# A decoder layer with a mixture of experts on one core: expert rows fetched one transfer per token tile, group maxima taken inside the normalisation loop, and a row broadcast issued behind the last router product

## The chip, the cores and the metric

The kernel runs on one core of one Trainium2 chip. The metric is the device time of one execution in microseconds; the median of the runs is quoted, and the profile comes from one execution of its own.

## What is computed

One hybrid decoder layer on 512 tokens of width 1024, in float32. The part up to the first normalisation is attention and a short convolution, joined by an output projection. After it:

```python
x = layer_norm(alpha * x + gate1 * mix, ln1_g, ln1_b)
h2 = x * (1 + scale2) + shift2
g = argmax(h2 @ w_router_group + b_router_group)        # 1 of 4 groups
e0, e1 = top 2 of the 8 experts of that group, by h2 @ w_router_expert + b
moe = sum over the two experts of weight * ((silu(h2 @ w_gate) * (h2 @ w_up)) @ w_down)
out = layer_norm(alpha * x + gate2 * moe, ln2_g, ln2_b)
```

There are 32 experts with 3 MB of weights each.

## The kernel before

Tokens are cut into four tiles of 128. Each engine has its own program, written out by hand, and they meet at semaphores.

**Output projection and first normalisation.** TensorE computes the projection in nine pieces (`project_out`, L1549; eight products of 512 or 256 columns each). VectorE takes each piece with `mix` (L1039). In a loop over the tiles (L1075 to L1099) it takes the moments, asks GpSimd for a power (`inv_std`, L613: the inverse deviation), computes the centred and scaled rows into `h2nat` meanwhile (L1081), waits for the power, and writes `h2p` (L1091). The last tile is written in two halves. ScalarE stores `h2p` to memory (`store_h2`, L808), normalises `xs` (L813) and copies the transposed rows out of PSUM into `h2T` (L829, L840 for the halves of the last tile).

**Router.** TensorE turns the rows (`transpose_h2`, L1560) and multiplies them by the router weights (`route`, L1570: eight products of 40 columns, two TensorE instructions each). Its order at the end of this stage, L1589 to L1602: transpose 0, projection piece 6, route 0, transpose 1, pieces 7 and 8, transpose 2, route 1, `spread_row(6)`, route 2, transpose 3, route 3. `spread_row` (L1542) is one 512-column product with a matrix of ones; it broadcasts half a row of `gate2` over the partitions and `row_out` (L795) on ScalarE copies it out. Rows 0 to 6 come before the choice of experts, row 7 after it.

VectorE chooses with `choose(first, n)` (L1102): first for tiles 0 to 2 together, then for tile 3. It adds the bias into `lg` (L1105), takes the group maximum and its index (L1108, L1111), masks the other groups, takes the two best experts, and ends with `mb` (L1129), the hot rows. TensorE sums these into positions (L1608), VectorE builds a table of slots (L1174 to L1178), TensorE multiplies it (L1618), VectorE turns the result into row numbers (L1164 to L1167), and GpSimd gathers the rows of the first expert pair (L627). TensorE fills that time with `spread_row(7)` and three more broadcasts whose results nobody reads (L1624). VectorE then finishes `xs` of tiles 3 and 2 (L1193, L1197), which signals `x1_last`.

**Weights.** SyncE issues all weight loads (L464 to L478) from a ring of 8 gate/up buffers of 2 MB (issued as two halves) and 6 down buffers of 1 MB. At the end of the router stage its order is: the load of expert 5 after the last logits (L503), the second half of buffer 7 after `x1_last` (L505), down weights 5, then expert 8 once the first expert's gate products are done.

**Experts.** Sixteen pairs; each expert takes gate/up products (L1640), a transpose, down products (L1649). Results go to `ysb`, and GpSimd scatters them to `y_dram`, whose row 2t + k holds token t's k-th expert.

**Tail.** When the last scatter but one has landed, SyncE loads the expert rows of each tile in the order 1, 2, 3, 0, one transfer of 512 KB for each of the two k (L541 to L544), with a semaphore for each. VectorE adds them to `x1`: `first_terms(1, 2)`, `(2, 2)`, `(3, 2)`, `(0, 1)` (L1359), each waiting for half k just before using it. TensorE adds the last pair's rows (L1759) and the partial sums (L1766), and for tile 0 also its second half (L1773). The statistics and the second normalisation follow, tile 1 on ScalarE and GpSimd, tiles 2, 3 and 0 on VectorE, and the output is stored.

Of the kernel before, what the change touches and what calls it, by code (L numbers as in the profile page):

```python
# [96 lines left out]
def layer_kernel(nc, x, c, w_ada, b_ada, w_in, conv_w, w_out, ln1_g, ln1_b, w_router_group,  # L97
# [3 lines left out]
    with ctx:  # L101
# [6 lines left out]
        def sem(name):  # L108
            return ctx.enter_context(nc.semaphore(name))
# [113 lines left out]

        lg = rtm("lg", [P, TC, NR])
        lem = rtm("lem", [P, TC, NE])
        g_top, e_top = rtm("g_top", [P, TC, 8]), rtm("e_top", [P, TC, 8])
        g_idx, e_idx = rtm("g_idx", [P, TC, 8], U32), rtm("e_idx", [P, TC, 8], U32)
        not_g = rtm("not_g", [P, TC, NG])
# [33 lines left out]
        ld_x1 = [sem(f"ld_x1{i}") for i in range(TC)]  # L262
        ld_y = [[sem(f"ld_y{i}{k}") for k in range(2)] for i in range(TC)]
        st_h2 = [sem(f"st_h2{n}") for n in range(2)]
# [144 lines left out]
        def _(sp):  # L409
# [131 lines left out]
            for i in TAIL:  # L541
                for k in range(2):
                    sp.dma_start(y_tok[i][:, k], y_dram.rearrange("(i p k) n -> i k p n", p=P, k=2)[i, k]
                                 ).then_inc(ld_y[i][k], 16)  # L544
            out_rows = out[0].rearrange("(i p) n -> i p n", p=P)
# [169 lines left out]
        def _(act):  # L715
# [103 lines left out]
            for i in range(TC - 1):  # L819
# [10 lines left out]
                if i == 1:  # L830
                    act.wait_ge(x1_done, 1)
                    store_x1(1)
            row_out(6)
            act.wait_ge(h2_done, TC + 1)
            store_h2(TC - 1)
            for half in range(2):
# [3 lines left out]
                s.copy(h2T_of(TC - 1)[:, ks].rearrange("p k t -> p (k t)"), flat[:, half * 512:(half + 1) * 512]).then_inc(h2t_ev, 1)  # L840
            normal(TC - 1)
            act.wait_ge(gap_done, 1)
            s.activation(g4[:, 1], g4[:, 0], ACT.Exp).then_inc(gap_exp, 1)
# [83 lines left out]
        def _(dve):  # L927
# [7 lines left out]
            def settle():  # L935

                dve.wait_ge(dve_did, count[0])
# [129 lines left out]
            def moments(n):  # L1067
# [5 lines left out]
                w.tensor_scalar(var_e[:, n:n + 1], mv[:, n, 1:2], EPS, None, ALU.add).then_inc(var_done, 1)  # L1073

            for i in range(TC):  # L1075
                wait(dve, h2_done, i)
                mix(TC + i)
                if i == TC - 1:
# [3 lines left out]
                                           op0=ALU.subtract, op1=ALU.mult))  # L1082
                if i >= 2:
                    dve.wait_ge(st_h2[i % 2], 16)
                    dve.wait_ge(h2t_done, i - 1)
# [16 lines left out]
            def choose(first, n):  # L1102

                tiles = slice(first, first + n)
                link(w.tensor_tensor(lg[:, tiles], ps[:, 2 + first // 3, first % 3 * NR:(first % 3 + n) * NR].rearrange("p (c e) -> p c e", c=n),  # L1105
                                     b_r[:].unsqueeze(1).to_broadcast([P, n, NR]), ALU.add))
                for i in range(first, first + n):
                    did(w.max(out=g_top[:, i], in_=lg[:, i, 0:GPAD]))  # L1108
                settle()
                for i in range(first, first + n):  # L1110
                    did(w.max_index(out=g_idx[:, i], in_max=g_top[:, i], in_values=lg[:, i, 0:GPAD]))  # L1111
                settle()
                link(w.tensor_tensor(not_g[:, tiles], iota[:, 0:NG].unsqueeze(1).to_broadcast([P, n, NG]),
# [17 lines left out]
            dve.wait_ge(h2_done, TC + 1)  # L1131
            dve.wait_ge(ld_br, 32)
            dve.wait_ge(pads, 2)
            dve.wait_ge(logit_done, TC - 1)
# [224 lines left out]
            def first_terms(i, n):  # L1359

                dve.wait_ge(ld_x1[i], 16)
                for k in range(n):
                    dve.wait_ge(ld_y[i][k], 16)
                    ins = w.scalar_tensor_tensor(out=x1_rows_of(i), in0=y_tok[i][:, k], scalar=wk[:, k, i:i + 1],
                                                 in1=x1_rows_of(i), op0=ALU.mult, op1=ALU.add)
                    if k + 1 < n:
                        link(ins)
                ins.then_inc(partial, 1)
# [22 lines left out]
        def _(pe):  # L1391
# [178 lines left out]
            def route(i, halves=1):  # L1570
                for half in range(halves):
                    pe.wait_ge(h2t_ev, i + 1 + half)
                    for k in range(half * KC // halves, (half + 1) * KC // halves):
                        ins = t.matmul(ps[:, 2 + i // 3, i % 3 * NR:(i % 3 + 1) * NR], h2T_of(i)[:, k], w_r[:, k],
                                       start=k == 0, stop=k == KC - 1)
                ins.then_inc(logit_done, 1)
# [18 lines left out]
            transpose_h2(2)  # L1595
            route(1)
            pe.wait_ge(gate2_moved, 1)
            pe.wait_ge(mixg_done, 2 * TC - 1)
            spread_row(6)
            route(2)  # L1600
            transpose_h2(3, halves=2)
            route(3, halves=2)  # L1602

# [158 lines left out]
            def other_terms(i, by_pe):  # L1762
# [7 lines left out]
                if by_pe:  # L1770
                    pe.wait_ge(ld_y[i][1], 16)
                    for n in range(2):
                        t.matmul(ps[:, sum_bank(i) + n], diag[:, i, 1], y_tok[i][:, 1, n * 512:(n + 1) * 512],  # L1773
                                 start=False, stop=True).then_inc(summed, 1)
# [36 lines left out]
```

## Time and profile before

| | |
|---|---|
| median of 3 runs | 551.34 us (550.74 to 553.63) |
| the profiled execution's own time | 551.43 us |
| its span, first to last instruction | 549.7 us |
| mean granted TensorE clock | 0.979 |
| TensorE busy | 509.2 us, 93% |
| VectorE busy | 285.4 us, 52% |
| HBM read / written | 159.60 MB / 17.30 MB, 322 GB/s over the span |

How to read the rows further down: times are microseconds from the start of the span. In the chain of waits each line is a piece of the one chain that ended last: start, length, what. In a timeline a line is a group of instructions that run on without a break: start, length, engine, line of the kernel, operation, output and input, count, and in brackets how long the engine was idle before it and what ended that. TensorE matmuls are listed with their start and a modelled end, so two groups in a row overlap a little. PEclk is the granted TensorE clock, 1.00 for 2.4 GHz and 0.50 for 1.2 GHz. SPq is SyncE issuing a transfer, ACTq is ScalarE doing so.

### The profile page before, as it was taken

Reading aid. Unit: us, or ns where it says so; the run is one execution under the profiler, and the core shown is the slowest. Engines: PE = TensorE matmul, PEld = TensorE weight load, DVE = VectorE, ACT = ScalarE, POOL = GpSimd, SP = SyncE. Lnnn points to the kernel's source line nnn. Section 1 sums busy time; section 2 is a strip of 40 time slices with the busy share of each in tenths; the row PEclk is TensorE's granted clock in tenths of the full one; section 3 lists DMA queues with packets and bytes.
Section 4 is the critical chain, followed back from the end, with each engine's and each line's share of the span. In section 5 each row is a group of like instructions: output and inputs, shape, how many; then the busy total and the mean of one; then the engine's idle time right before and its main releaser. Section 6 shows DMA issues by size and latency. Waiting matters only on the chain.

```text
span 549.7 us, 6477 instructions
## 1 busy us (share of the span) xinstructions
PE 509.2 (93%) x2516; PEld 275.4 (50%) x2516; DVE 285.4 (52%) x520; ACT 105.5 (19%) x173; POOL 102.8 (19%) x112
## 2 busy tenths in 40 slices
PE   3999999999999999999996999999998798899883
PEld 2445468744444444444584555555554354444531
DVE  4675999664946393263888732232222222213388
ACT  1000211233122321100232311111111111122020
POOL 2000000061316040030452111111211021111115
PEclk9999999999999999999996999999999999979997
DMA  8999779944640254269998999999999999999863
GB/s 258 357 360 352 229 240 317 317 172 153 229 154 1 78 171 158 66 258 418 410 385 317 397 407 422 414 415 418 415 416 419 414 415 416 416 417 416 308 239 153
DMA packets 71296, 169.22 MB, mean 308 GB/s; under 512 B 7918, under 2 KB 45858, under 8 KB 63072
## 3 DMA queue, kind: packets, MB, share of 16 engines
q1 hardware_dynamic: 64304, 152.22, 73.4%
q10 hardware_dynamic: 2480, 8.44, 4.0%
q0 software_dynamic: 4480, 8.12, 3.9%
q8 instruction: 21, 0.34, 0.2%
q14 instruction: 11, 0.09, 0.0%
HBM read 159.60 MB, written 17.30 MB: 322 GB/s over the span
## 4 chain that ended last, share of the span: by engine, by line
PE 75%; DVE 9%; DMA 9%; SPq 3%; issue 3%; ACT 1%; POOL 0%; DVEq 0%; POOLq 0%; ACTq 0%
PE ps L1640 17%; PE ps L1510 11%; PE ps L1556 10%; PE ps L1649 8%; PE ps L1421 8%; PE ps L1480 5%; DMA w_gu<-in_w_up_dram 5%; PE ps L1630 3%; PE ps L1473 2%; DMA y_tok<-y_dram 2%; PE ps L1499 2%; PE ps L1544 2%; SPq L466 1%; DVE acc_rows L954 1%; DMA xs<-in_x_dram 1%
## 5 line engine op out<-in xcount | busy, mean ns | idle before, releaser
L1640 PE MATMUL ps<-w_gu,xT 128*64 128x256 f32 x1024 | 119.4, 386 | 6.0 <-issue 3.1
L1640 PEld LDWEIGHTS ps<-w_gu,xT 128*64 128x64 f32 x1024 | 72.4, 138 | 43.5 <-issue 5.8
L1510 PE MATMUL ps<-hT,w_stage 128*128 128x512 f32 x192 | 84.8, 595 | 0.0
L1275 DVE TENSOR_TENSOR ysb<-ps,rows_gate 64x512 f32<-64x512 f32 x64 | 44.1, 688 | 58.6 <-PE ps L1649 58.1
L1649 PE MATMUL ps<-w_dn,hidT 128*64 128x512 f32 x256 | 61.4, 599 | 6.3 <-issue 5.6
L1266 DVE TENSOR_TENSOR hid<-ps,silu_sb 128x128 f32<-128x128 f32 x32 | 9.3, 292 | 94.3 <-ACT silu_sb L865 94.3
L954 DVE SCALAR_TENSOR_TENSOR acc_rows<-ada_stage,csil,acc_rows 128x256 f32<-128x256 f32 x112 | 55.2, 493 | 4.0
L1510 PEld LDWEIGHTS ps<-hT,w_stage 128*128 128x128 f32 x192 | 35.5, 190 | 41.0 <-issue 41.0
L1556 PE MATMUL ps<-wo,mixT 128*128 128x512 f32 (+1 forms) x144 | 55.6, 545 | 0.0
L1421 PE MATMUL ps<-hT,w_first 128*128 128x512 f32 x96 | 45.9, 625 | 0.9 <-DVE hT L980 0.9
L1556 PEld LDWEIGHTS ps<-wo,mixT 128*128 128x128 f32 x144 | 27.2, 190 | 27.1 <-issue 26.3
L640 POOL DMA_INDIRECT y_dram<-ysb,slot_row x14 | 14.2, 1012 | 141.2 <-DVE ysb L1275 141.2
L1649 PEld LDWEIGHTS ps<-w_dn,hidT 128*64 128x64 f32 x256 | 17.0, 136 | 29.1 <-issue 24.6
L865 ACT ACTIVATE silu_sb<-ps 128x128 f32<-128x128 f32 x32 | 8.9, 278 | 114.0 <-PE ps L1640 114.0
L1421 PEld LDWEIGHTS ps<-hT,w_first 128*128 128x128 f32 x96 | 18.2, 199 | 20.0 <-issue 20.0
L1480 PE MATMUL ps<-w_stage,hT 128*128 128x256 f32 x128 | 27.8, 379 | 0.0
L1002 DVE TENSOR_TENSOR_SCAN stay<-stay,block_end 128x1280 f32<-128x1280 f32 x8 | 24.1, 3014 | 4.2 <-POOL stay L592 4.2
L1480 PEld LDWEIGHTS ps<-w_stage,hT 128*128 128x128 f32 x128 | 24.3, 190 | 3.7 <-issue 0.5
L589 POOL TENSOR_SCALAR_AFFINE_SELECT stay<-stay 128x384 f32<-128x384 f32 x8 | 5.3, 659 | 100.5 <-ACT stay L746 100.5
L627 POOL DMA_INDIRECT xg<-h_dram,slot_tok x16 | 16.9, 1054 | 37.1 <-PE ps L1640 23.1
L966 DVE SCALAR_TENSOR_TENSOR acc_cols<-ada_in,csil,acc_cols 128x512 f32<-128x512 f32 (+1 forms) x35 | 22.6, 645 | 1.5 <-DMA ada_in<-in_w_ada_dram 0.2
L1044 DVE TENSOR_TENSOR h2nat<-ps,rows_gate 128x512 f32<-128x512 f32 (+1 forms) x9 | 5.7, 631 | 25.1 <-PE ps L1556 25.0
(221 smaller groups left out, 513.5 us busy)
## 6 DMA issues: line engine op xcount, KB each, us to landing
w_gu<-in_w_gate_dram SPq DMA_DIRECT2D x32, 1024.0 KB, 19.9
w_gu<-in_w_up_dram SPq DMA_DIRECT2D x32, 1024.0 KB, 23.0
w_dn<-in_w_down_dram SPq DMA_DIRECT2D x32, 1024.0 KB, 24.5
ada_stage<-in_w_ada_dram SPq DMA_DIRECT2D x16, 1024.0 KB, 6.3
w_stage<-in_w_in_dram SPq DMA_DIRECT2D x9, 1024.0 KB, 8.4
ada_in<-in_w_ada_dram SPq DMA_DIRECT2D x12, 512.0 KB, 9.4
y_dram<-zeros ACTq DMA_DIRECT2D x4, 1024.0 KB, 5.8
wo<-in_w_out_dram SPq DMA_DIRECT2D x2, 2048.0 KB, 12.1
```

Source lines behind the costliest of these rows:

```text
L627: g.indirect_dma_start(out=buf[:], out_offset=None, in_=h2_dram, in_offset=bass.IndirectOffsetOnAxis(ap=slot_tok[:, j:j + 1], axis=0), bou ...
L954: link(w.scalar_tensor_tensor(out=acc, in0=st[:, k], scalar=csil[:, 3, k:k + 1], in1=acc, op0=ALU.mult, op1=ALU.add))
L966: ins = w.scalar_tensor_tensor(out=acc, in0=ada_in[c][:, k], scalar=csil[:, 3, k:k + 1], in1=acc, op0=ALU.mult, op1=ALU.add)
L1002: w.tensor_tensor_scan(out=st[:, 0:ZW][:, ::-1], data0=st[:, 0:ZW][:, ::-1], data1=block_end[:, ::-1], initial=1.0, op0=ALU.mult, op1=ALU. ...
L1275: ins = w.tensor_tensor(to[e * HD:(e + 1) * HD, b * 512:(b + 1) * 512], ps[b * HD:(b + 1) * HD, down_bank(y), :], gate2r[b * HD:(b + 1) * ...
L1421: ins = t.matmul(ps[:, n], w_first[:, k, n * P:(n + 1) * P], hT[:, k], start=k == 0, stop=k == KC - 1)
L1480: ins = t.matmul(dst[:, 0:CW], hT[:, k, i * P:(i + 1) * P], st[:, k], start=k == 0, stop=k == KC - 1)
L1510: ins = t.matmul(ps[:, 6], st[:, k, (f % 2) * P:(f % 2 + 1) * P], hT[:, k], start=k == 0, stop=k == KC - 1)
L1556: ins = t.matmul(ps[:, 4 + q % 4, 0:width], mixT[:, i, k], wo[n][:, k, col:col + width], start=k == 0, stop=k == KC - 1)
L1630: ins = t.transpose(flat[:, ROWS_AT + k * P:ROWS_AT + (k + 1) * P], by_channel(xg[rows_buffer(j)])[:, k], ident[:])
L1640: ins = t.matmul(ps[a * SLOTS:(a + 1) * SLOTS, GATE_BANK[e], 0:2 * P], rows_in[:, k, e * SLOTS:(e + 1) * SLOTS], weights[:, :, k, a * P:(a ...
L1649: ins = t.matmul(ps[b * SLOTS:(b + 1) * SLOTS, bank, :], hidT[e][:, a * SLOTS:(a + 1) * SLOTS], weights[:, a, b * 512:(b + 1) * 512], star ...
```

## The change

Three edits. (1) The expert rows of a tile come in one transfer of 1 MB, with one semaphore, instead of two of 512 KB; `first_terms` waits for it before its first use. (2) The group maximum of one tile becomes a function `group_top`. It is called for tile 0 in the loop at i = 2 and for tile 1 at i = 3, behind the computation of `h2nat` and ahead of the wait for the power; `choose` calls it for its last tile only (tile 2, then tile 3). For this the buffers `lg`, `g_top` and `g_idx` get a place of their own, the waits for the bias move ahead of the loop, and the logits of even tiles go to PSUM bank 2, of odd tiles to bank 3. (3) `spread_row(6)` moves on TensorE from behind route 1 to behind route 3, and `row_out(6)` on ScalarE from ahead of the last tile's copies to behind `normal(3)`.

```diff
-        lg = rtm("lg", [P, TC, NR])
+        lg = sm("lg", [P, TC, NR])
...
-        g_top, e_top = rtm("g_top", [P, TC, 8]), rtm("e_top", [P, TC, 8])
-        g_idx, e_idx = rtm("g_idx", [P, TC, 8], U32), rtm("e_idx", [P, TC, 8], U32)
+        g_top, e_top = sm("g_top", [P, TC, 8]), rtm("e_top", [P, TC, 8])
+        g_idx, e_idx = sm("g_idx", [P, TC, 8], U32), rtm("e_idx", [P, TC, 8], U32)
...
             for i in TAIL:
-                for k in range(2):
-                    sp.dma_start(y_tok[i][:, k], y_dram.rearrange("(i p k) n -> i k p n", p=P, k=2)[i, k]
-                                 ).then_inc(ld_y[i][k], 16)
+                sp.dma_start(y_tok[i][:], y_dram.rearrange("(i p k) n -> i p k n", p=P, k=2)[i]).then_inc(ld_y[i], 16)
...
-            row_out(6)
             act.wait_ge(h2_done, TC + 1)
             store_h2(TC - 1)
...
             normal(TC - 1)
+            row_out(6)
             act.wait_ge(gap_done, 1)
...
+            def group_top(i):
+
+                link(w.tensor_tensor(lg[:, i], ps[:, 2 + i % 2, i // 2 * NR:(i // 2 + 1) * NR], b_r[:], ALU.add))
+                link(w.max(out=g_top[:, i], in_=lg[:, i, 0:GPAD]))
+                link(w.max_index(out=g_idx[:, i], in_max=g_top[:, i], in_values=lg[:, i, 0:GPAD]))
+
+            dve.wait_ge(ld_br, 32)
+            dve.wait_ge(pads, 2)
             for i in range(TC):
...
                 if i >= 2:
+                    dve.wait_ge(logit_done, i - 1)
+                    group_top(i - 2)
                     dve.wait_ge(st_h2[i % 2], 16)
...
-                link(w.tensor_tensor(lg[:, tiles], ps[:, 2 + first // 3, first % 3 * NR:(first % 3 + n) * NR].rearrange("p (c e) -> p c e", c=n),
-                                     b_r[:].unsqueeze(1).to_broadcast([P, n, NR]), ALU.add))
-                for i in range(first, first + n):
-                    did(w.max(out=g_top[:, i], in_=lg[:, i, 0:GPAD]))
-                settle()
-                for i in range(first, first + n):
-                    did(w.max_index(out=g_idx[:, i], in_max=g_top[:, i], in_values=lg[:, i, 0:GPAD]))
-                settle()
+                group_top(first + n - 1)
...
                 dve.wait_ge(ld_x1[i], 16)
+                dve.wait_ge(ld_y[i], 16)
                 for k in range(n):
-                    dve.wait_ge(ld_y[i][k], 16)
...
             transpose_h2(2)
             route(1)
+            route(2)
+            transpose_h2(3, halves=2)
+            route(3, halves=2)
             pe.wait_ge(gate2_moved, 1)
             pe.wait_ge(mixg_done, 2 * TC - 1)
             spread_row(6)
-            route(2)
-            transpose_h2(3, halves=2)
-            route(3, halves=2)
```

## Rows read from the trace of the kernel before

**Rows 1.** Chain of waits, expert stage: start us, us, what.

```profile
440.01 25.28 DMA w_gu<-in_w_up_dram
```

**Rows 2.** Chain of waits, end of projection to the first expert rows.

```profile
281.95 0.88 PE ps L1567 x8
...
284.54 0.93 PE ps L1544 x2
285.47 1.73 PE ps L1574 x16
...
287.32 0.29 DVE lg L1105
...
290.72 0.12 DVE lg L1105
...
292.62 0.17 DVE mb L1129
...
295.71 2.01 PE ps L1544 x2
```

**Rows 3.** SyncE's own waits, 280 to 306 us: total, times, longest.

```profile
SPq L466 <- DVE ps L1197: 9.8, 1, 9.8
```

**Rows 4.** Timeline, all engines, last tile's rows and logits.

```profile
283.79 1.28 DVE L1081 SCALAR_TENSOR_TENSOR h2nat<-xs,mv,rows_a 128x1024 f32<-128x1024 f32 x1
283.95 1.52 POOL L613 TENSOR_TENSOR rstd<-var_e,mh 128x1 f32<-128x1 f32 x1 [4.50 <-DVE var_e L1073]
285.68 1.41 DVE L1091 SCALAR_TENSOR_TENSOR h2p<-h2nat,rstd,rows_b 128x512 f32<-128x512 f32 x2 [0.62 <-POOL rstd L613]
287.13 0.33 ACTq L809 DMA_DIRECT2D h_dram<-h2p  x1
287.73 1.07 ACT L840 COPY h2T<-ps 128x512 f32<-128x512 f32 x2 [1.63 <-PE ps L1567]
288.36 1.98 PE L1574 MATMUL ps<-w_r,h2T 128*128 128x40 f32 x16 [0.23 <-ACT h2T L840]
291.35 0.16 DVE L1113 TENSOR_TENSOR not_g<-iota,g_idx 128x4 f32<-128x4 f32 x1
...
295.16 0.22 ACT L843 ACTIVATE g<-g 128x16 f32<-128x16 f32 x1 [3.93 <-DVE g L1180]
```

**Rows 5.** Windows: us, PE, PEld, DVE, ACT, POOL busy, PEclk, DMA share, GB/s.

```profile
290.00:291.00 1.00, 0.34 (x4) 0.22 (x2) 0.90 (x6) 1.00 (x1) 0.00 (x0) 0.83 0.98 279
...
300.00:301.00 1.00, 1.00 (x3) 0.42 (x2) 1.00 (x2) 0.00 (x0) 0.44 (x1) 0.55 0.46 172
...
481.50:482.00 0.50, 0.50 (x2) 0.07 (x1) 0.00 (x0) 0.38 (x1) 0.42 (x1) 0.81 1.01 418
```

**Rows 6.** Chain of waits, one-row broadcasts of the second norm's rows.

```profile
479.35 4.83 PE ps L1690 x8
```

**Rows 7.** Timeline, SyncE's loads of the expert rows and VectorE's first two terms.

```profile
516.52 6.14 SPq L543 DMA_DIRECT2D y_tok<-y_dram  x8
...
524.70 1.29 DVE L1364 SCALAR_TENSOR_TENSOR x_back<-y_tok,wk,x_back 128x1024 f32<-128x1024 f32 x1
...
526.83 1.28 DVE L1364 SCALAR_TENSOR_TENSOR x_back<-y_tok,wk,x_back 128x1024 f32<-128x1024 f32 x1 [0.85 <-DMA y_tok<-y_dram]
```

**Rows 8.** Line 543, the last of the eight loads: duration ns, start; issue to landing.

```profile
L543 SPq DMA_DIRECT2D y_tok<-y_dram x1: 933/933/933, 521.7 to 521.7; - x1
...
DMA to landing us min/median/max: 12.6/12.6/12.6
```

**Rows 9.** Chain of waits in the tail.

```profile
528.30 1.30 DVE x_sb L1364
...
533.34 1.28 DVE x_back L1364
```

**Rows 10.** Windows in the tail, columns as in rows 5.

```profile
524.00:526.00 2.00, 1.28 (x3) 0.68 (x4) 1.95 (x2) 0.00 (x0) 0.00 (x0) 1.00 1.01 297
526.00:528.00 2.00, 2.00 (x6) 0.76 (x4) 1.17 (x1) 0.00 (x0) 0.00 (x0) 1.00 1.00 389
```

More of the change, by code:

```diff
@@ L222, in rtm @@
             return at(name, shape, o, dt)
-        lg = rtm("lg", [P, TC, NR])
+        lg = sm("lg", [P, TC, NR])
         lem = rtm("lem", [P, TC, NE])
-        g_top, e_top = rtm("g_top", [P, TC, 8]), rtm("e_top", [P, TC, 8])
-        g_idx, e_idx = rtm("g_idx", [P, TC, 8], U32), rtm("e_idx", [P, TC, 8], U32)
+        g_top, e_top = sm("g_top", [P, TC, 8]), rtm("e_top", [P, TC, 8])
+        g_idx, e_idx = sm("g_idx", [P, TC, 8], U32), rtm("e_idx", [P, TC, 8], U32)
+        assert base + small[0] <= nc.sbuf_usable_end
         not_g = rtm("not_g", [P, TC, NG])
@@ L262, in layer_kernel @@
         ld_x1 = [sem(f"ld_x1{i}") for i in range(TC)]
-        ld_y = [[sem(f"ld_y{i}{k}") for k in range(2)] for i in range(TC)]
+        ld_y = [sem(f"ld_y{i}") for i in range(TC)]
         st_h2 = [sem(f"st_h2{n}") for n in range(2)]
@@ L1131, in _ @@
             dve.wait_ge(h2_done, TC + 1)
-            dve.wait_ge(ld_br, 32)
-            dve.wait_ge(pads, 2)
             dve.wait_ge(logit_done, TC - 1)
@@ L1573, in route @@
                     for k in range(half * KC // halves, (half + 1) * KC // halves):
-                        ins = t.matmul(ps[:, 2 + i // 3, i % 3 * NR:(i % 3 + 1) * NR], h2T_of(i)[:, k], w_r[:, k],
+                        ins = t.matmul(ps[:, 2 + i % 2, i // 2 * NR:(i // 2 + 1) * NR], h2T_of(i)[:, k], w_r[:, k],
                                        start=k == 0, stop=k == KC - 1)
@@ L1770, in other_terms @@
                 if by_pe:
-                    pe.wait_ge(ld_y[i][1], 16)
+                    pe.wait_ge(ld_y[i], 16)
                     for n in range(2):
```

## The prediction

> **What bounds the kernel now.** I read the chain of waits first, then the windows with the granted clock, then the timelines of the two stretches that the change touches.
>
> In the expert stage the chain rests on weight loads; the longest piece is one of 25.28 us [rows 1]. A delay of TensorE alone is swallowed there. What is not swallowed is the moment at which the stream of loads starts again after the router. SyncE waited 9.8 us for VectorE's last sum of `xs` before it could issue the second half of buffer 7 [rows 3], and the transfer engines are only half busy meanwhile, at 300 to 301 [rows 5]. That sum hangs on the choice of experts. So a microsecond in the choice is a microsecond at the end, through the stream of loads.
>
> In the router the chain runs on TensorE to the end of route 2 at 287.20, then through VectorE's two choices: tiles 0 to 2 from 287.32, tile 3 from about 290.64 (the second addition into `lg` overlaps the end of the first choice), `mb` ready at 292.79 [rows 2]. The logits of tile 3 ended at 288.36 + 1.98 = 290.34 [rows 4]: 0.3 us before they were needed. Of the 3.3 us of the first choice, then, little more than 0.3 can be taken away before route 3 decides.
>
> In the tail VectorE adds seven blocks of 1.28 us; it waited 0.85 us for tile 1's second half [rows 7], and from 528.30 on it goes at its own pace, 5.04 us for four blocks, to 533.34 [rows 9].
>
> **The change, part by part.**
>
> *Group maxima in the loop.* One tile's addition, maximum and index take VectorE from 290.64 to 291.35, 0.71 us [rows 2, 4]. At i = 3 `h2nat` ends at 285.07 and the power at 285.47, `h2p` starts at 285.68 [rows 4]: a hole of 0.62 us. With the addition overlapping the end of `h2nat` by 0.08, as it does in rows 2, `group_top` ends at 285.70. The hole covers all but some hundredths; I take 0.05 for each of the two calls, 0.1 in all, at most 0.2. The power itself is covered by nothing new: GpSimd starts it before. Queued behind the new wait for logits is `h2p`, but route 1 ended at 284.54 [rows 2], before `h2nat` does. Route 0 is earlier still, and the bias landed before the loop. In `choose` two of three tiles' maxima go: about 0.5 us, plus 0.2 because it may start at the end of `h2p`.
>
> *The broadcast behind route 3.* Route 2 moves up by 0.93 us, to 284.54 to 286.27 [rows 2]. Transpose 3 no longer stands behind it but waits for `h2p`: first half at 286.4 + 0.1. ScalarE can copy only after it has issued the store of `h2p`, at 287.13 + 0.33, about 287.5 [rows 4], where it copied at 287.73. Route 3 thus starts 0.2 us earlier at best. With the 0.1 from above, the choice of tile 3 starts at 290.3 instead of 290.64: a gain of 0.3 us. The bound is then route 3, with VectorE waiting for it. The broadcast itself (0.93 us) hides in the 2.5 us in which TensorE waits for `mb`. On ScalarE the copy of row 6 now stands ahead of the exponential, which ran at 295.16 after ScalarE had waited 3.93 us for VectorE [rows 4]; that wait covers it. SyncE's load of expert 5 waits for route 3 too, and goes with it.
>
> *The clock, which this reordering touches.* The granted clock fell from 2.4 to 1.2 GHz at 290.66 (0.83 in the window 290 to 291) and came back at 300.9 [rows 5]. Before the fall TensorE had done nothing wider than 128 columns since the broadcast ended at 285.47, 5.2 us earlier [rows 2]. Between the router and the tail it fell once more, at 481.81 (0.81 in the window 481.5 to 482), 2.5 us after TensorE had begun the one-row broadcasts of the second norm [rows 5, 6]. In the new order the broadcast no longer stands between routes 1 and 2: the last wide product ends at 281.95 [rows 2]. Then come a transpose, route 1, route 2, transpose 3 and route 3, all narrow. With the longer of the two lags the clock falls at 287.2, with the shorter at 284.5. Either is ahead of route 3. I take 287.2, from the row nearest to this case in kind.
>
> What does it cost? No row shows the 40-column products at 1.2 GHz. Nothing at all is the lower bound, twice the time the upper. The same two 512-column instructions took 0.93 us at the high clock and 2.01 at the low [rows 2], so I take twice. The first half of transpose 3 stays fast. The second starts at 287.2 and takes 0.85 us instead of 0.43, the last copy ends near 289.0, which still leads its half of route 3. Route 3: start 288.15, 2 × 1.71 = 3.42 us, and the 0.27 us by which the modelled end lags [rows 2, 4]: 291.85. The choice of tile 3 starts at 292.0 instead of 290.64: **+1.3 us**. `mb` comes at 294.1; the broadcast, now slow, ends at about 293.3 and still hides. The gather and the broadcasts that fill its time move with VectorE.
>
> *One transfer per tile.* VectorE's first block of tile 1 ran at 524.70 while the second half was under way [rows 7]; now both blocks start when the whole tile is there. Where does it land? If 1 MB lands when its second half did, at 526.83, tile 2 starts at 526.83 + 2.52 = 529.35 instead of 528.30: +1.05 us [rows 7, 9]. Tile 0 must be there whole, too: its second half landed at 521.7 + 12.6 = 534.3 [rows 8], while VectorE took its first half at 533.34 [rows 9]: +1.0 again, at the same place, so not added. The other bound: in 524 to 526 the engines were fully busy but moved 297 GB/s, afterwards 389 [rows 10]. If larger pieces take away that slow time, the tile lands at about 525.1 and VectorE gains 0.7 us. The second of these rows shows that today's pieces run fast as well once the slow time is over, so I stay above the middle and take **+0.5**. Four issues of 0.8 us on average (6.14 for eight) go from SyncE [rows 7], but the first one starts as before, and the later ones were not what the data waited for.
>
> The Trainium skill, page "DMA: Bandwidth & Descriptors", section "Rules for kernel authors", asks for at least 1 MiB in a DMA for the best bandwidth and for many small transfers to be joined. By that rule the merged load would land earlier, and the tail term would be the lower bound instead of the one taken.
>
> *Sum*: 551.43 + 1.3 + 0.5 = **553.2 us**. The profiled execution stands 0.09 above the median of the three runs, so the same number serves against either.
>
> **The rivals.**
>
> *The clock holds through route 3.* For it: the fall before came only after route 3, when TensorE already stood still, so that the idle time and not the narrow work may have brought it. Then the router gives -0.3, the tail +0.5: 551.6. Chance 0.24.
>
> *The transfer gains.* The slow time in rows 10 goes and tile 1 lands at 525.1: router +1.3, tail -0.7, so 552.0 (550.4 where the clock holds too). Against it: the tail's last loads landed about as fast as VectorE used them. Chance 0.18. The skill's rule above speaks for this one.
>
> *Slower: the clock falls during route 2.* With the short lag, as in rows 5 and 6, it falls at 284.5 to 284.8. Route 2 then ends at 287.7, the transposes at 289.45, the first copy at 289.5, route 3 at 289.5 + 3.42 + 0.27 = 293.2; the choice of tile 3 starts at 293.3, +2.65. With the tail: 554.6. It decides if the fall comes before 286.27, the end of route 2. Chance 0.15.
>
> *The change does nothing that shows.* The two effects are too small beside the spread of the runs, or the stream of loads takes up the router's delay: -0.3 to +0.5, 551.4. Against it: SyncE's wait [rows 3]. This shares the first rival's numbers; chance 0.05.
>
> The forecast itself has 0.38.
>
> **How the numbers follow.** Half a per cent, 2.8 us, is about what a measurement of this kernel can tell from no change. The forecast and three rivals lie inside it. Slower takes about 0.12 of the early fall and 0.05 of the forecast (the clock term at its worst with +1.0 in the tail gives 554.0 and above). Faster would need over 548.6; only the transfer rival with both favourable terms comes near, 0.03. The range goes from 550.4, that pair, to 554.8, the early fall.
>
> **What would show it.** In the windows PEclk at 0.50 from about 287 and route 3 taking about 3.5 us; VectorE idle for about 2 us ahead of the second choice, released by L1574; `x1_last` and the load behind it 1.3 us later; in the tail VectorE idle from 524.7 (plus the shift) until the first tile lands, then seven blocks nearly without a break. The forecast is wrong if PEclk is 1.00 until 290 or later, if route 3 takes about 1.7 us at 1.2 GHz, or if VectorE starts its first block of the tail before 525 (plus the shift).

## The result, and the profile after

The changed kernel takes 553.79 us in the median of 20 executions (552.78 to 556.48). The kernel before takes 551.38 (550.22 to 553.83, 20 executions). The ratio is 1.0043, 95% interval 1.0032 to 1.0055: 2.4 us slower, 1.8 to 3.0. That lies inside the half per cent that was named for "the same", and is yet a loss that the interval keeps from zero.

| | before | after |
|---|---|---|
| profiled execution, own time | 551.43 us | 556.14 us |
| its span | 549.7 us | 554.3 us |
| mean granted TensorE clock | 0.979 | 0.969 |
| projection's last product ends | 281.95 | 283.15 |
| choice of tile 3 starts | 290.64 | 293.32 |
| second half of weight buffer 7 issued | 301.01 | 303.71 |
| gate products of expert 30 | 509.59, 3.67 us | 512.41, 5.36 us |
| last `ysb` complete | 524.66 | 529.17 |

The profiled execution of the changed kernel stands 2.35 us above its median. Two pieces of its difference lie outside the code that the change touches: 1.2 us before the router, and 1.7 us in the gate products of expert 30. Both parts hold a stretch at 1.2 GHz that the profile of the kernel before does not show; it is told of further down. So I measure the router from the end of the projection: 8.69 us to the choice of tile 3 before, 10.17 after, **+1.48 us**.

The first view is the timeline of TensorE, VectorE and ScalarE in the changed kernel, from the normalisation of the last tile to its choice; it answers to [rows 2, 4].

```profile
283.86 3.66 PE L1574 MATMUL ps<-w_r,h2T 128*128 128x40 f32 x32
...
286.25 0.19 DVE L1076 TENSOR_TENSOR lg<-ps,b_r 128x40 f32<-128x40 f32 x1
...
286.76 0.16 DVE L1078 FIND_INDEX8 g_idx<-g_top,lg 128x8 uint32<-128x8 f32 x1
287.07 1.41 DVE L1100 SCALAR_TENSOR_TENSOR h2p<-h2nat,rstd,rows_b 128x512 f32<-128x512 f32 x2
287.97 1.86 PE L1567 MATMUL ps<-ident,h2p 128*128 128x128 f32 x8 [0.45 <-DVE h2p L1100]
288.51 0.20 DVE L1076 TENSOR_TENSOR lg<-ps,b_r 128x40 f32<-128x40 f32 x1
289.01 0.58 ACT L838 COPY h2T<-ps 128x512 f32<-128x512 f32 x1 [3.94 <-PE ps L1567]
...
289.65 3.64 PE L1574 MATMUL ps<-w_r,h2T 128*128 128x40 f32 x16
...
293.09 2.05 PE L1544 MATMUL ps<-rows_gate,ones 128*128 128x512 f32 x2
293.32 0.20 DVE L1076 TENSOR_TENSOR lg<-ps,b_r 128x40 f32<-128x40 f32 x1 [1.89 <-PE ps L1574]
...
295.55 0.29 PE L1608 MATMUL ps<-mb,before 128*128 128x128 bf16 x1 [0.41 <-DVE mb L1131]
```

Routes 1 and 2 stand as one group of 32 products in 3.66 us. Route 3, half as many, takes 3.64. VectorE, which went from one choice straight into the other before, now idles 1.89 us until L1574 ends. The broadcast moved behind it, 293.09 to 295.14, ends before `mb` releases L1608: it is hidden, as forecast. What is slow is the work it left behind. The windows of the changed kernel, columns as in [rows 5], show why:

```profile
288.00:288.50 0.50, 0.50 (x3) 0.50 (x4) 0.48 (x1) 0.00 (x0) 0.00 (x0) 0.66 1.05 442
290.00:291.00 1.00, 1.00 (x7) 1.00 (x6) 0.93 (x10) 1.00 (x2) 0.00 (x0) 0.50 1.11 410
```

PEclk is 0.66 over 288.0 to 288.5: it went from 1.00 to 0.50 at about 288.16, 5.0 us after the projection's last wide product, ahead of route 3. Here TensorE is without a pause in the window at 290, and at 1.2 GHz.

SyncE's own waits in the changed kernel (total, times, longest) answer to [rows 3]:

```profile
SPq L467 <- DVE ps L1197: 8.8, 1, 8.8
SPq L467 <- PE ps L1574: 8.0, 1, 8.0
```

Together the two waits grew from 16.0 us (9.8 and 6.2) to 16.8, and both end later. The load behind them is issued 10.39 us after the choice of tile 3, 10.37 before. The delay goes through to the stream of loads undiminished.

The tail: VectorE's timeline and, from the view of line 543, the loads of the expert rows, answering to [rows 7, 8].

```profile
527.78 1.39 DVE L1275 TENSOR_TENSOR ysb<-ps,rows_gate 64x512 f32<-64x512 f32 x2 [1.16 <-PE ps L1649]
529.21 2.60 DVE L1364 SCALAR_TENSOR_TENSOR x_back<-y_tok,wk,x_back 128x1024 f32<-128x1024 f32 x2
531.73 5.11 DVE L1364 SCALAR_TENSOR_TENSOR x_sb<-y_tok,wk,x_sb 128x1024 f32<-128x1024 f32 x4
536.76 1.28 DVE L1364 SCALAR_TENSOR_TENSOR x_back<-y_tok,wk,x_back 128x1024 f32<-128x1024 f32 x1
...
541.55 1.29 DVE L1339 BATCH_NORM_STATS2 bn<-ps 128x6 f32<-128x512 f32 x2 [0.47 <-PE ps L1766]
```

```profile
L543 SPq DMA_DIRECT2D y_tok<-y_dram x4: 320/433/652, 518.5 to 519.8; - x4
...
DMA to landing us min/median/max: 9.5/12.6/15.5
```

Tile 1, the first, is whole 9.5 us after its issue at 518.47, at 528.0. VectorE is busy with `ysb` until 529.17 and finds it there. The seven blocks run without a wait. Two lines of the chain of waits show what is late next: TensorE's sums, which in this execution begin with `ysb`.

```profile
529.23 3.70 PE ps L1759 x8
...
539.80 1.73 PE ps L1766 x4
```

From the last `ysb` to the end of the span it is 25.04 us before and 25.13 after. That near equality hides two pieces, and the fourteen profiles of all kernels part them. The first runs from the last `ysb` to the last two instructions of VectorE (L1351): 20.62 to 20.64 us in all eight profiles with one transfer per tile, 20.62 to 20.63 in four with two, but 20.90 and 21.11 in the other two (`undo_transfer` and the kernel before), where a second half came late. The second runs from there to the end of the span: 4.42 to 4.50 us in all eight with one transfer, 3.83 to 3.93 in all six with two. The last output store, 256 KB of tile 0, lands 2.6 us after its issue in the eight and 2.0 in the six. The medians over the two halves of tile 0 show it, before and after:

```profile
out_dram<-x_back SPq DMA_DIRECT2D x2, 256.0 KB, 2.0
out_dram<-x_back SPq DMA_DIRECT2D x2, 256.0 KB, 2.4
```

So edit 1 costs some 0.55 us behind the last instruction of VectorE, and the profile of before hides it, since its second half was 0.5 us late. In the eight profiles one packet of 8 KB of queue 14 (kind: instruction) runs beside that last store, at 552.39 us in the changed kernel. In the six it comes at 523 to 530 us. That it holds the store up is argued; no run moves it alone.

### The profile page after: what moved, and what is told of

It is laid out like the page before. It is cut to its first block, busy times and chain, and to the rows that moved or that the text cites. A ratio compares the mean times of both kernels' runs of the same rounds, so it can differ in the third digit from the quotient of the medians.

```text
span 554.3 us, 6472 instructions
## 1 busy us (share of the span) xinstructions
PE 514.6 (93%) x2516; PEld 278.0 (50%) x2516; DVE 286.0 (52%) x522; ACT 105.5 (19%) x173; POOL 102.0 (18%) x112
## 3 DMA queue, kind: packets, MB, share of 16 engines
q10 hardware_dynamic: 2480, 8.44, 4.0%
## 4 chain that ended last, share of the span: by engine, by line
PE 73%; DVE 11%; DMA 7%; SPq 5%; issue 3%; ACT 1%; POOL 1%; DVEq 0%; POOLq 0%; ACTq 0%
PE ps L1640 19%; PE ps L1510 11%; PE ps L1649 9%; PE ps L1556 7%; PE ps L1421 6%; PE ps L1480 5%; DMA w_gu<-in_w_up_dram 4%; PE ps L1630 3%; PE ps L1473 2%; PE ps L1499 2%; SPq L421 2%; DMA ada_in<-in_w_ada_dram 2%; DVE acc_rows L953 1%; PE ps L1759 1%; PE ps L1658 1%
## 5 line engine op out<-in xcount | busy, mean ns | idle before, releaser
L1640 PE MATMUL ps<-w_gu,xT 128*64 128x256 f32 x1024 | 120.7, 389 | 6.0 <-issue 3.7
L1649 PE MATMUL ps<-w_dn,hidT 128*64 128x512 f32 x256 | 62.8, 612 | 6.5 <-issue 5.8
L1630 PEld LDWEIGHTS ps<-ident,xg 128*128 128x128 f32 x128 | 15.5, 194 | 7.1 <-issue 5.8
```

The costliest lines, as they stand in the source:

```text
L1630: ins = t.transpose(flat[:, ROWS_AT + k * P:ROWS_AT + (k + 1) * P], by_channel(xg[rows_buffer(j)])[:, k], ident[:])
L1640: ins = t.matmul(ps[a * SLOTS:(a + 1) * SLOTS, GATE_BANK[e], 0:2 * P], rows_in[:, k, e * SLOTS:(e + 1) * SLOTS], weights[:, :, k, a * P:(a ...
L1649: ins = t.matmul(ps[b * SLOTS:(b + 1) * SLOTS, bank, :], hidT[e][:, a * SLOTS:(a + 1) * SLOTS], weights[:, a, b * 512:(b + 1) * 512], star ...
```

## The experiments

A ratio is to the kernel before, timed on the same chip, with its 95% interval. "Router" is the time from the end of the projection to the choice of tile 3, in the profile: 8.69 us before.

### Edit 3 alone: `only_broadcast`, `only_broadcast_again`

```diff
@@ the kernel before, TensorE (ScalarE: row_out(6) behind normal(3))
             route(1)
-            pe.wait_ge(gate2_moved, 1)
-            pe.wait_ge(mixg_done, 2 * TC - 1)
-            spread_row(6)
             route(2)
             transpose_h2(3, halves=2)
             route(3, halves=2)
+            pe.wait_ge(gate2_moved, 1)
+            pe.wait_ge(mixg_done, 2 * TC - 1)
+            spread_row(6)
```

> The kernel before with the third edit alone: the broadcast of row 6 behind route 3, its copy behind normal(3). Theory (the clock): the last wide product ends before route 1, PEclk is at 0.50 during route 3, route 3 takes about 3.5 us instead of 1.7, the choice of tile 3 starts 1.0 to 1.5 us later, and the time is 1.0 to 2.3 us above before (ratio 1.002 to 1.004). Rival (the order alone): moving the broadcast only lets route 2 run 0.9 us earlier; the time is 0 to 0.5 us below before, and the loss of the whole change lies in the tail.

Measured: 1.0016 (0.9996 to 1.0036), just under the ratio that was expected, 0.9 us in the medians; router 9.92 us, +1.23. The timeline of TensorE and VectorE:

```profile
283.54 3.66 PE L1574 MATMUL ps<-w_r,h2T 128*128 128x40 f32 x32
287.46 1.58 PE L1567 MATMUL ps<-ident,h2p 128*128 128x128 f32 x8 [0.25 <-DVE h2p L1091]
289.07 3.64 PE L1574 MATMUL ps<-w_r,h2T 128*128 128x40 f32 x16
...
292.75 0.20 DVE L1105 TENSOR_TENSOR lg<-ps,b_r 128x40 f32<-128x40 f32 x1 [1.33 <-PE ps L1574]
```

The slow route 3 needs nothing but this move. The interval still touched 1, so the same kernel ran once more, on another chip.

> The kernel before with the third edit alone, for a second set of times. Theory (the broadcast alone makes nearly the whole loss): ratio 1.002 to 1.004, route 3 takes about 3.5 us. Rival (each of the three edits adds its part, the broadcast only 0.9 us): ratio 1.0010 to 1.0018.

Measured: 1.0026 (1.0010 to 1.0042), and again a router of 9.92 us with route 3 in 3.64. The move alone costs 0.9 to 1.3 us in the medians; the trace says 1.23.

### Edit 1 alone: `only_transfer`

```diff
-                for k in range(2):
-                    sp.dma_start(y_tok[i][:, k], ...[i, k]).then_inc(ld_y[i][k], 16)
+                sp.dma_start(y_tok[i][:], ...[i]).then_inc(ld_y[i], 16)
```

> The kernel before with the first edit alone: one transfer of 1 MB per token tile. Theory: VectorE starts its first block later but the tile lands up to 1 us sooner after its issue than the second half did; the time is between 0.3 us below and 0.6 us above before. Rival (the load is the loss): VectorE stands idle for 2 us after its last ysb and the time is 1 us or more above before. Rival (larger pieces help): 0.7 us or more below before.

Measured: 0.9999 (0.9980 to 1.0018). VectorE's timeline in the tail:

```profile
523.07 1.39 DVE L1273 TENSOR_TENSOR ysb<-ps,rows_gate 64x512 f32<-64x512 f32 x2 [1.16 <-PE ps L1647]
525.01 2.60 DVE L1362 SCALAR_TENSOR_TENSOR x_back<-y_tok,wk,x_back 128x1024 f32<-128x1024 f32 x2 [0.55 <-DMA y_tok<-y_dram]
527.53 2.60 DVE L1362 SCALAR_TENSOR_TENSOR x_sb<-y_tok,wk,x_sb 128x1024 f32<-128x1024 f32 x2
```

The wait moved from between the two blocks to ahead of both, and is shorter: 0.55 us for 0.85 [rows 7] and the 0.18 of this row of the kernel before:

```profile
528.30 5.12 DVE L1364 SCALAR_TENSOR_TENSOR x_sb<-y_tok,wk,x_sb 128x1024 f32<-128x1024 f32 x4 [0.18 <-DMA y_tok<-y_dram]
```

VectorE takes the whole of tile 1 9.33 us after the first issue at 515.68, and begins tile 2 11.85 us after it. Before, it took the second half of tile 1 after 10.31 us and began tile 2 after 11.78. So the larger piece is there 1.0 us sooner than the second of two halves was. VectorE has to wait for all of it where it could begin with the first half, and the two cancel. From the last `ysb` to the end it is 25.04 us, as in the profile before, but in two pieces that moved apart: 20.62 us for 21.11 to the last instructions of VectorE, 4.42 for 3.93 behind them, with the last store landing 2.6 us after its issue for 2.0.

The Trainium skill, page "DMA: Bandwidth & Descriptors", section "Rules for kernel authors", asks for 1 MiB and more and for joined transfers. The trace agrees as far as the landing goes (1.0 us sooner) and the kernel's time does not follow (0.9999).

### Edit 2 alone: `only_maxima`

```diff
                 if i >= 2:
+                    dve.wait_ge(logit_done, i - 1)
+                    group_top(i - 2)
@@ choose
-                (sum over all tiles, max and max_index of each tile)
+                group_top(first + n - 1)
```

> The kernel before with the second edit alone: group maxima of tiles 0 and 1 taken in the loop, with their buffers and the two PSUM banks. Theory: the two calls hide behind the power but for 0.1 us, the first choice is shorter by 0.5 us, and route 3 then decides: 0.1 to 0.3 us below before, ratio 0.9990 to 1.0005. Rival: VectorE's additional links delay the last rows by 0.3 us or more, and the time is above before by as much.

Measured: 0.9994 (0.9975 to 1.0013), router 8.45 us, -0.24. VectorE's timeline:

```profile
286.81 0.20 DVE L1078 TENSOR_TENSOR lg<-ps,b_r 128x40 f32<-128x40 f32 x1
...
289.52 0.21 DVE L1133 TENSOR_TENSOR mb<-oh 128x96 bf16<-128x96 bf16 x1
289.89 0.20 DVE L1078 TENSOR_TENSOR lg<-ps,b_r 128x40 f32<-128x40 f32 x1 [0.16 <-PE ps L1576]
```

From the first `lg` of the choice to `mb` it is 2.71 us instead of 3.19. Then VectorE waits 0.16 us for route 3: as the prediction has it, the gain ends where route 3 decides. A quarter of a microsecond is less than the timing resolves.

### The whole change less edit 3: `undo_broadcast`

```diff
@@ the changed kernel, TensorE (ScalarE: row_out(6) back ahead of the copies)
             route(1)
+            pe.wait_ge(gate2_moved, 1)
+            pe.wait_ge(mixg_done, 2 * TC - 1)
+            spread_row(6)
             route(2)
             transpose_h2(3, halves=2)
             route(3, halves=2)
-            pe.wait_ge(gate2_moved, 1)
-            pe.wait_ge(mixg_done, 2 * TC - 1)
-            spread_row(6)
```

> The changed kernel with the third edit undone: the broadcast is back between routes 1 and 2, its copy ahead of the last tile's store. Theory (the clock): route 3 runs at 2.4 GHz in most executions and takes 1.7 us, the time is within 0.5 us of before (ratio 0.999 to 1.001), so 2 us below the changed kernel. Rival (the tail or the maxima are the loss): it stays 1.5 us or more above before.

Measured: 0.9990 (0.9973 to 1.0008), router 8.44 us. The timeline of TensorE and VectorE:

```profile
284.48 1.10 PE L1544 MATMUL ps<-rows_gate,ones 128*128 128x512 f32 x2
...
288.49 1.98 PE L1574 MATMUL ps<-w_r,h2T 128*128 128x40 f32 x16 [0.25 <-ACT h2T L839]
...
290.50 0.20 DVE L1076 TENSOR_TENSOR lg<-ps,b_r 128x40 f32<-128x40 f32 x1 [0.16 <-PE ps L1574]
```

With the broadcast back, route 3 takes 1.98 us and the whole loss is gone. Edits 1 and 2 keep their place and give nothing that the timing can tell.

### The changed kernel again, and less each of the other edits: `after_again`, `undo_transfer`, `undo_maxima`

The first kernel has no edit. In the second, edit 1 is undone:

```diff
-                sp.dma_start(y_tok[i][:], ...[i]).then_inc(ld_y[i], 16)
+                for k in range(2):
+                    sp.dma_start(y_tok[i][:, k], ...[i, k]).then_inc(ld_y[i][k], 16)
```

In the third, edit 2, with its buffers and PSUM banks:

```diff
-                    dve.wait_ge(logit_done, i - 1)
-                    group_top(i - 2)
```

> The changed kernel once more, on the same chip as the three that follow. Both theories: 1.5 to 3 us above before (ratio 1.003 to 1.0055).

> The changed kernel with the first edit undone: two transfers per tile again, maxima in the loop, broadcast behind route 3. Theory (the transfer costs nothing that shows, the clock is the loss): route 3 takes about 3.5 us, the choice of tile 3 starts 1.3 to 1.6 us later than before, counted from the end of the projection, and the time is 1.2 to 2.4 us above before. Rival (the transfer costs about a microsecond together with the late router, since the whole change lost 2.4 us and the broadcast alone 0.9): 0.5 to 1.2 us above before, at least 1 us below the changed kernel.

> The changed kernel with the second edit undone: one transfer per tile and the broadcast behind route 3, the maxima all in the choice. Theory (the broadcast is the loss, the maxima and the transfer cost some tenths each at most): route 3 takes 3.5 us, the choice of tile 3 starts 1.2 us later than before counted from the end of the projection, the time is 0.9 to 2.0 us above before (ratio 1.0016 to 1.0036). Rival (the maxima cost by themselves once TensorE is at 1.2 GHz): it stays within 0.6 us of before.

| | ratio | router us | route 3 us |
|---|---|---|---|
| `after_again` | 1.0048 (1.0029 to 1.0066) | 10.11 | 3.63 |
| `undo_transfer` | 1.0029 (1.0015 to 1.0043) | 10.24 | 3.64 |
| `undo_maxima` | 1.0040 (1.0027 to 1.0053) | 9.93 | 3.64 |

Each of these kernels has edit 3, is slower than before, and has the slow route 3. The router shows that the edits do not add up: edit 2 gains 0.24 us alone, but beside edit 3 it costs 0.2 to 0.3 (10.11 to 10.24 us with both, 9.92 and 9.93 without edit 2). Route 3 then decides alone, and what `group_top` adds ahead of `h2p` is added to it. Without edit 1 the loss may be smaller by a third (1.3 us below `after_again` in the medians, as the rival of its expectation has it), but the intervals overlap. VectorE's timeline of `undo_transfer` shows the tail as it was before, with the wait for the second half:

```profile
527.66 1.28 DVE L1366 SCALAR_TENSOR_TENSOR x_back<-y_tok,wk,x_back 128x1024 f32<-128x1024 f32 x1
529.63 1.28 DVE L1366 SCALAR_TENSOR_TENSOR x_back<-y_tok,wk,x_back 128x1024 f32<-128x1024 f32 x1 [0.69 <-DMA y_tok<-y_dram]
```

From the last `ysb` to the end it takes 24.77 us, 0.36 less than the changed kernel. The other profiles with two transfers bear this out: 24.46 to 24.54 us in `only_broadcast`, its repeat, `only_broadcast_unread` and `only_maxima`, and 25.04 in the kernel before alone, beside 25.04 to 25.13 in the eight with one transfer. By these traces edit 1 costs between 0 and 0.6 us, and mostly 0.5. The timing agrees and cannot narrow it: five pairs of kernels that differ in edit 1 alone range from 0.2 us faster to 1.3 us slower with one transfer, by their ratios, and the intervals of each pair overlap.

### The clock itself: `unread_wide`, `only_broadcast_unread`

If route 3 is slow only because TensorE did nothing wide before it, one more wide product, whose result nobody reads, must give the time back although it is more work. In the changed kernel, and likewise in the kernel with edit 3 alone, where the waits stay behind route 3 too:

```diff
             route(1)
+            pe.wait_ge(gate2_moved, 1)
+            pe.wait_ge(mixg_done, 2 * TC - 1)
+            t.matmul(ps[:, ROW_BANK[6]], ones[:], gate2r[:, 0:512], start=True, stop=True)
             route(2)
             transpose_h2(3, halves=2)
             route(3, halves=2)
-            pe.wait_ge(gate2_moved, 1)
-            pe.wait_ge(mixg_done, 2 * TC - 1)
             spread_row(6)
```

> The changed kernel with one 512-column product more, whose result nobody reads, between routes 1 and 2, where the broadcast stood; the broadcast itself stays behind route 3 and its copy behind normal(3). TensorE has more work than in either kernel. Theory (the clock): PEclk stays 1.00 through route 3 in most executions, route 3 takes 1.7 us, the time is within 0.5 us of before (ratio 0.999 to 1.001). Rival (the place of the broadcast or of its copy on ScalarE costs by itself): the time stays 1.5 us or more above before, or above the changed kernel.

> The kernel before with the third edit and one unread 512-column product between routes 1 and 2: only_broadcast with more work for TensorE. Theory (the clock): route 3 takes 1.7 us, the time is within 0.5 us of before and 0.5 to 1.5 us below only_broadcast's 552.5. Rival (the new place of the broadcast and of its copy costs by itself): at only_broadcast's level or above.

Measured: 1.0003 (0.9988 to 1.0017) and 0.9996 (0.9985 to 1.0006). TensorE's timeline and a window of `unread_wide`:

```profile
284.39 1.10 PE L1599 MATMUL ps<-rows_gate,ones 128*128 128x512 f32 x2
285.34 1.87 PE L1574 MATMUL ps<-w_r,h2T 128*128 128x40 f32 x16
287.04 1.12 PE L1567 MATMUL ps<-ident,h2p 128*128 128x128 f32 x8
288.41 1.98 PE L1574 MATMUL ps<-w_r,h2T 128*128 128x40 f32 x16 [0.25 <-ACT h2T L838]
290.22 1.10 PE L1544 MATMUL ps<-rows_gate,ones 128*128 128x512 f32 x2
```

```profile
290.00:291.00 1.00, 1.00 (x6) 0.49 (x5) 0.73 (x6) 0.00 (x0) 0.00 (x0) 1.00 0.90 229
```

The broadcast stands behind route 3, as in the change, and TensorE has 0.95 us more to do. PEclk is 1.00 at 290 and route 3 takes 1.98 us. The same in the other kernel: 

```profile
284.17 1.10 PE L1599 MATMUL ps<-rows_gate,ones 128*128 128x512 f32 x2
...
288.17 1.98 PE L1574 MATMUL ps<-w_r,h2T 128*128 128x40 f32 x16 [0.23 <-ACT h2T L839]
```

The move as such costs nothing that the timing can tell. What costs is that the projection and route 3 have nothing wide between them any more. That is shown: one product of no use to the result (two TensorE instructions) takes the ratio from 1.0048 to 1.0003 in the changed kernel, against the same runs of before. No run put narrow work of the same length in its place, so that it is the width of the product, and not the 0.95 us more of work, rests on the six profiles in which some 5 us of narrow products did not hold the clock.

### The broadcast between route 2 and transpose 3: `broadcast_mid`, `broadcast_mid_again`

```diff
@@ the changed kernel
             route(2)
+            pe.wait_ge(gate2_moved, 1)
+            pe.wait_ge(mixg_done, 2 * TC - 1)
+            spread_row(6)
             transpose_h2(3, halves=2)
             route(3, halves=2)
-            pe.wait_ge(gate2_moved, 1)
-            pe.wait_ge(mixg_done, 2 * TC - 1)
-            spread_row(6)
```

> The changed kernel with the broadcast between route 2 and transpose 3 instead of behind route 3; its copy stays behind normal(3). Route 2 still moves up, transpose 3 starts about where it did before, and the last wide product is 1.7 us later than before. Theory (the clock): the clock falls only when TensorE stands still after route 3, which takes 1.7 us in all executions; 0.2 to 0.8 us below before (ratio 0.9985 to 0.9997). Rival (the clock has nothing to do with the last wide product): route 3 takes 3.5 us in some executions and the time is above before.

> The same kernel as broadcast_mid, for a second profile and its times. Theory (the clock may fall within the 4.3 us of narrow products that now lead up to the broadcast, so that route 3 runs slow in part of the executions): about 1 us above before again, and PEclk at 0.50 ahead of route 3 if this profile catches it. Rival (the first result was by chance, with an early fall of the clock near 29 us in that execution): the time is at or below before.

Measured: 1.0024 (1.0012 to 1.0036) and 1.0015 (1.0002 to 1.0029), a miss: I had looked for a gain. Yet both profiles have the fast route 3. TensorE's timeline of the second:

```profile
282.81 3.66 PE L1574 MATMUL ps<-w_r,h2T 128*128 128x40 f32 x32
286.30 1.10 PE L1544 MATMUL ps<-rows_gate,ones 128*128 128x512 f32 x2
...
288.54 1.98 PE L1574 MATMUL ps<-w_r,h2T 128*128 128x40 f32 x16 [0.24 <-ACT h2T L838]
```

The first profile has its router at 8.45 us, faster than before, and reached it 1.1 us later, with a stretch at 1.2 GHz near 30 us. The second shows no loss at all: its own time is 551.64 us, beside medians of 551.89 for this kernel and 551.68 for before. Neither caught what the other executions lose. Up to 0.6 us of it can be edit 1, which both contain: their tails take 25.12 us. That the clock falls in some executions during the 4.3 us of narrow products ahead of the broadcast is an argument, not a finding. It stays open.

No kernel here beats the one before: the lowest ratios, of `undo_broadcast` (0.9990), `only_maxima` (0.9994) and `only_broadcast_unread` (0.9996), have intervals that hold 1.

## Why the prediction was right, and where it was off

The forecast was 553.2 us, within half a per cent, by a clock that falls ahead of route 3. The median is 553.79, in the range, and the mechanism of the larger term, the clock, is the one that was forecast. That the number came within 0.6 us is in part luck: the term for the transfer is about right in size for a reason that was not forecast, and part of the measured loss has no term. The steps:

**The maxima hide.** The two calls of `group_top` delay `h2p` by 0.19 us (it starts 3.92 us after the projection, 3.73 before), where I took 0.1 and allowed 0.2. The choice of tiles 0 to 2 is shorter by 0.48 us, as forecast, and in `only_maxima` the net gain is 0.24, where 0.1 to 0.3 was expected.

**The clock falls ahead of route 3.** Forecast 5.2 us after the last wide product; measured 5.0 here, 5.2 in `after_again`, 5.3 and 5.5 in the two profiles with edit 3 alone. The choice of 287.2 over 284.5 was right: route 2 was never touched.

**Its price.** "Twice the time" held: 3.64 us for route 3 (3.69 forecast) beside 1.98, and 1.86 for the transposes beside 1.05 to 1.12. The choice of tile 3 was forecast 10.05 us after the projection and came after 10.17 and 10.11. Route 3 began 6.50 us after the projection, forecast 6.20: 0.1 of this is `h2p`, and ScalarE's copy, which I had following the store of `h2p` at once, started 0.17 us after that was issued. VectorE followed sooner on its end than I had allowed, which gave about half of it back. The term is +1.48 and +1.42, where the sum had +1.3.

**It goes through to the end.** SyncE's load keeps its distance to the choice (10.37, 10.39 us). The route by which the stream of loads could have swallowed the delay stayed closed.

**The transfer, +0.5.** The step that failed is that VectorE would start tile 2 later: "The second of these rows shows that today's pieces run fast as well once the slow time is over, so I stay above the middle". From the issue to the start on the whole tile took 9.33 us in `only_transfer`, between the two bounds (8.6 and 10.3), and tile 2 began 0.07 us later, not 0.5. The lower bound itself, 525.1, was worked out from no row. The engines moved, in windows of the changed kernel with columns as in [rows 5],

```profile
524.00:526.00 2.00, 1.65 (x9) 0.48 (x7) 0.87 (x3) 0.27 (x1) 0.00 (x0) 1.00 0.98 401
```

401 GB/s, where they moved 297 before [rows 10]. The loads of the changed kernel were issued 2 us later; `only_transfer`, whose loads were not, moved 430 from 523 to 525 us. The sign that I had named, VectorE idle until the first tile lands, is there in `only_transfer` (0.55 us) and not in the changed kernel, whose `ysb` was later. What the forecast did not have is the last output store, which lands 2.6 us after its issue for 2.0 in every profile with one transfer per tile. So edit 1 costs 0 to 0.6 us of the 0.5 forecast, and does it at another place.

**What the sum does not hold.** The trace of the router gives +1.48 us, the transfer 0 to 0.6, the timing +2.4 (1.8 to 3.0). The rest is some 0.3 to 0.9 us of the 2.4, and may be nothing at the low end of the interval. I can place but not settle it. Both profiles of the changed kernel show one more low stretch, in the gate products of expert 30. TensorE's timeline of the changed kernel:

```profile
508.39 1.94 PE L1649 MATMUL ps<-w_dn,hidT 128*64 128x512 f32 x8 [0.35 <-ACT hidT L858]
512.41 5.36 PE L1640 MATMUL ps<-w_gu,xT 128*64 128x256 f32 x32 [2.08 <-issue]
```

5.36 us for what takes 3.67 otherwise: +1.7. These two executions took 556.14 and 554.85 us. The 20 of the changed kernel lie in two heaps, 11 from 552.8 to 553.9 and 9 from 554.89 up; of before, 15 lie below 552.0 and 5 from 553.0 up. A low stretch that costs 1.7 us, in more of the executions than before, would make both the heaps and the rest. The mean granted clock of the executions does not part the heaps: 0.966 to 0.983 in the lower, 0.966 to 0.972 in the upper. But `only_maxima`, which is as fast as before, has the 5.36 us too in its profile, and no execution of the lower heap was profiled. Whether the change makes this stretch more frequent stays open.

**The rivals.** "The clock holds" is out by the windows of every kernel with edit 3 whose wide product is gone. "The transfer gains" is out by the traces: tile 2 began 0.07 us later in `only_transfer` and the last store landed 0.6 us later. Its timing, 0.9999 (0.9980 to 1.0018), could not have told a gain of 0.7 us from none. "The clock falls during route 2" happened in none of six such profiles; its sum is 554.6, and the range was drawn to 554.8 for it. "Nothing shows" is out by the interval.

## What to carry to other kernels

When a wide product is moved away from a stretch of narrow ones to fill a hole elsewhere, read the granted clock of the stretch it leaves: the time may not be in the product but in what it did for its neighbours. Price such a move with the narrow work at half the clock, and test it with one wide product that nobody reads in the old place; if the time comes back with more work, it was the clock. Two halves on which the consumer can start one after the other were worth about as much here as the sooner landing of one joined transfer. And compare the tail over every profile at hand, down to the landing of the last store: two profiles alone, 25.04 and 25.13 us, showed no loss where the others show half a microsecond.

## What the runs showed of the hardware that was not expected

- From the end of the projection to the fall of the clock TensorE had one pause, of 0.25 to 0.46 us, and was otherwise busy with transposes of 128 columns and products of 40. The clock fell all the same, 5.0 to 5.5 us after the last product of 256 columns, in all six profiles with nothing wide in between. A single 512-column product in between put it off until route 3 was done, in all eight others.
- Low stretches come in some executions of a kernel and not in others. The clock was at 1.2 GHz from about 28.8 to 32.2 us in the profile of the changed kernel and not in that of the same kernel run again; the projection ended at 283.15 and 281.97. Three experiments show the same near 28 to 33 us. Not all of the 1.2 us need be the stretch: without one, the projection of `only_broadcast` ended at 282.83. The Trainium skill, page "TensorE: Matmul & The Clock Gate", section "What's actually happening", says that the point at which the clock changes varies from run to run; the trace agrees, with the 5.0 to 5.5 us above. That a whole stretch is there in one execution and missing in the next, that sentence does not say.
- Ahead of the gate products of expert 30 TensorE idles either 2.06 to 2.09 us (eight of the fourteen profiles) or 1.24 to 1.34 us (six). The clock fell during these products in three of the eight and in none of the six.
- With one transfer per tile in place of two, a packet of 8 KB of queue 14 (kind: instruction) came beside the last output store, and that store landed 2.6 us after its issue for 2.0, in eight of eight profiles against none of six. Fewer transfers issued by one engine went with a change some 30 us further on, in code that was not touched.
